# Output projection of a hybrid decoder layer: activations held in the array, 512 weight columns moving

## What is computed

```python
mixed = concat([a * silu(ga), p * silu(gb)], axis=-1)           # 544 x 2048
h = (DEEPNORM_ALPHA * x + einsum('btc,cd->btd', mixed, w_out))  # w_out 2048 x 2048
mu = mean(h); var = mean(square(h - mu))
y = (h - mu) * rsqrt(var + LN_EPS) * ln_g + ln_b
```

## Time and profile before

| | |
|---|---|
| median of 3 runs | 1218.41 us |
| the profiled execution | 1214.59 us |
| its span in the trace | 1212.5 us |
| matmuls busy | 1179.9 us, 97% |
| first matmul of stage D | 983.23 us |
| last matmul of stage D ends | 1186.75 us |

### The profile page before, as it was taken

One profiled execution on the slowest core, in us unless ns is written; L12 is line 12 of the kernel. 1 busy time (PEld: TensorE's weight loads), 2 busy tenths in 40 slices (PEclk: granted clock), 3 DMA queues, 4 the chain that ended last, 5 costly groups with the idle time before them and its releaser, 6 DMA issues.

```text
span 1212.5 us, 26754 instructions
## 1 busy us (share of the span) xinstructions
PE 1179.9 (97%) x10300; PEld 1087.3 (90%) x10300; DVE 597.2 (49%) x1083; ACT 359.0 (30%) x665; POOL 354.1 (29%) x150
## 2 busy tenths in 40 slices
PE   6999999999999999999989999999999999999995
PEld 6888889999999999999987889888889879999992
DVE  3666658874665657451444622623523552323226
ACT  4333333223323323322333322322323342122210
POOL 2432222333333334334311311311321223333310
PEclk9999999999999999999999999999999999999996
DMA  7543143233232223354226857857867656222203
GB/s 250 130 121 80 48 111 89 70 88 89 79 104 82 80 79 98 93 154 129 62 85 196 287 208 245 300 194 250 287 207 248 214 189 219 82 76 86 69 1 147
DMA packets 197975, 170.50 MB, mean 141 GB/s; under 512 B 19890, under 2 KB 178538, under 8 KB 196658
## 3 DMA queue, kind: packets, MB, share of 16 engines
q1 hardware_dynamic: 184458, 160.48, 42.7%
q10 hardware_dynamic: 13424, 8.67, 2.4%
HBM read 159.47 MB, written 9.74 MB: 140 GB/s over the span
## 4 chain that ended last, share of the span: by engine, by line
PE 91%; DVE 6%; issue 1%; DMA 1%; ACT 1%; DVEq 0%; SPq 0%; ACTq 0%
PE acc L1138 67%; PE bank L1438 5%; PE bank L1454 3%; PE acc L1525 3%; PE bank L1196 2%; PE bank L1332 2%; PE bank L1313 2%; DVE scoreP L1793 1%; PE acc L1579 1%; DVE top L1789 1%; PE acc L1483 1%; DMA xnat<-in_x_prompt 1%; PE bank L1248 1%; DVE y L2185 1%; PE bank L1322 1%
## 5 line engine op out<-in xcount | busy, mean ns | idle before, releaser
L634 POOL TENSOR_TENSOR wL<-rawW,wH 128x1024 fp32r<-128x1024 f32 (+1 forms) x146 | 353.9, 2425 | 811.4 <-ACT wH L656 811.4
L1138 PE MATMUL acc<-actH,wH 128*128 128x272 f32 (+1 forms) x2304 | 491.5, 294 | 1.2 <-DVE actL L1707 1.2
L1138 PE MATMUL acc<-actH,wL 128*128 128x272 f32 (+1 forms) x2304 | 476.6, 288 | 0.0
L1138 PE MATMUL acc<-actL,wH 128*128 128x272 f32 (+1 forms) x2304 | 475.0, 288 | 0.0
L1138 PEld LDWEIGHTS acc<-actH,wH 128*128 128x128 f32 (+1 forms) x2304 | 360.1, 188 | 23.9 <-issue 21.9
L1138 PEld LDWEIGHTS acc<-actL,wH 128*128 128x128 f32 (+1 forms) x2304 | 361.4, 188 | 0.0
L1138 PEld LDWEIGHTS acc<-actH,wL 128*128 128x128 f32 (+1 forms) x2304 | 359.1, 188 | 0.0
L656 ACT ACTIVATE wH<-rawW 128x1024 fp32r<-128x1024 f32 (+1 forms) x146 | 153.7, 1054 | 226.2 <-PE acc L1138 210.3
L2120 DVE SCALAR_TENSOR_TENSOR y<-y,bank 128x512 f32 (+1 forms) x16 | 11.0, 688 | 122.3 <-PE bank L1647 120.4
L1438 PE MATMUL bank<-sq,kPage 128*128 128x128 f32 x480 | 65.6, 280 | 4.1 <-DVE kPT L1951 4.0
L1438 PEld LDWEIGHTS bank<-sq,kPage 128*128 128x128 f32 x480 | 52.9, 142 | 14.5 <-issue 9.8
(11 more groups left out here) (207 smaller groups left out, 1019.6 us busy)
## 6 DMA issues: line engine op xcount, KB each, us to landing
rawW<-in_w_in SPq DMA_DIRECT2D x112, 512.0 KB, 3.8
vPage<-in_cache_v SPq DMA_DIRECT2D x64, 512.0 KB, 4.8
kPage<-in_cache_k SPq DMA_DIRECT2D x60, 512.0 KB, 4.6
rawW<-in_w_out SPq DMA_DIRECT2D x32, 512.0 KB, 4.1
y<-in_x_prompt SPq DMA_DIRECT2D x4, 1024.0 KB, 9.3
out_y_prompt<-y SPq DMA_DIRECT2D x8, 512.0 KB, 2.8
xnat<-in_x_prompt SPq DMA_DIRECT2D x2, 1024.0 KB, 7.9
xnat<-in_x_prompt ACTq DMA_DIRECT2D x2, 1024.0 KB, 10.9
```

The lines of the kernel that those rows point to most:

```text
L634: pool.tensor_tensor(wL[:, slot, :, 0:width], rawW[:, slot, :, 0:width], wH[:, slot, :, 0:width].bitcast(F32), ALU.subtract).then_inc(stag ...
L1138: last = pe.matmul(acc[t.slot][0:width, e, 0:HT], w[:, u.slot, k, 0:width], a[:, kk, e * HT:(e + 1) * HT], start=(half == 0 and k == 0 and ...
```

## The change

In the output projection the operands change places. The activations of one token tile (128 channels by 128 tokens) are the stationary operand, and 512 weight columns move. The output has 4 blocks of 512 columns (`BLOCKS`, `WIDE`). A weight unit is now 2 chunks by 512 columns, still 512 KB, 8 units to a block, in the order `PAIRS`. For each unit and each of the 4 prompt token tiles there are 2 x 3 = 6 matmuls of 512 columns; the sums lie in four banks of PSUM, tokens on the partitions, and no transposes follow.

The 32 samples are not taken in three products but in one fp32 product of `mixed` with `rawW`: `sample_parts` puts 128x32 weights into the four column groups, one chunk to each, with 512 columns of `rawW` moving, once for each two units. The four partial sums stand on 128 partitions; ACT copies them out (`part_copy`), and `folded` adds them by a matmul with four identities side by side (`fold`, 128x32). As TensorE now reads `rawW`, SP waits for `pair_done` of the two units that had the slots before, where it waited for POOL; ACT waits for `pair_done` too.

The first eight units are taken in the last pass of `group` and after it, where `first_tile` was. On SP the units 4 to 7 of `w_out` stand after the pages of V and ahead of the loads of x. `gbc` has memory of its own.

In the last block the token tiles end one after another, and DVE, ACT and TensorE do the normalization of a tile while TensorE multiplies for the next: `normal`, `finished`, `shift_turned`, `correction`, in the order `NORMED` (tiles 0, 1, samples, 2, 3).

```diff
+WIDE = 4 * P
+BLOCKS = D // WIDE
+PAIRS = (4, 5, 6, 7, 0, 1, 2, 3)
+NORMED = (0, 1, TT, 2, 3)
...
+            def load_out_unit(t, n, col, done):
+                if done is None:
+                    sp.wait_ge(stage_ready[t.slot], t.free)
+                else:
+                    sp.wait_ge(pair_done, done)
+                stand_alone(sp)
+                sp.dma_start(rawW[:, t.slot].rearrange("p k c -> p (k c)").rearrange("p (k c) -> p k c", k=2),
+                             wo_view[:, 2 * PAIRS[n]:2 * PAIRS[n] + 2, ds(col, WIDE)]).then_inc(w_landed[t.slot], 16)
...
-                    load_unit(wo_view, 1 - half, (tile - 4) * P, t)
+                    load_out_unit(t, j - 8, 0, None if j < 12 else (j - 12) // 2 + 1)
...
                 for m in range(PAGES):
-                    if m % 2 == 0:
+                    if m % 2 == 0 and not last:
                         unit(12 + m // 2, last, g)
...
             group(LOOPS, True)
+            for j in range(12, 16):
+                unit(j, True, LOOPS)
...
-                for j in range(2):
-                    load_tile(wo_view, (2 * i + 4 + j) * P, TILE_D + 4 + j, i, 2)
+                for n in range(8):
+                    load_out_unit(turn(2 * TILE_D + 8 + n, 4, i, 8), n, (i + 1) * WIDE, 4 * i + (n + 4) // 2 + 1)
...
+            def out_high(n):
+                u = out_unit(n)
+                act.wait_ge(w_landed[u.slot], 16 * u.full)
+                act.wait_ge(pair_done, (n - 4) // 2 + 1)
+                act.activation(wH[:, u.slot, :, :], rawW[:, u.slot, :, :], ACT.Copy).then_inc(high_ready[u.slot], 1)
...
+            for n in range(4, 8 * BLOCKS):
+                if n % 8 == 2 and n > 8:
+                    part_copy(n // 8 - 1)
+                out_high(n)
...
+            def rows_times(q, t, n, first=False, last=False):
+                for c in range(2):
+                    k = 2 * PAIRS[n % 8] + c
+                    for w, parts in ((wH, (actH, actL)), (wL, (actH,))):
+                        for a in parts:
+                            end = pe.matmul(out_bank(q), a[:, k, t * P:(t + 1) * P], wide(w, n, c),
+                                            start=first and c == 0 and w is wH and a is actH,
+                                            stop=last and c == 1 and w is wL)
...
+            def sample_parts(p):
+                q = 5 * (p // 4) + TT
+                weights_ready(2 * p + 1)
...
+                for j in range(4):
+                    n, c = 2 * p + j // 2, j % 2
+                    end = pe.matmul(out_bank(q)[NS * j:NS * (j + 1), :], mixed[:, 2 * PAIRS[n % 8] + c, NP_:T], wide(rawW, n, c),
+                                    start=p % 4 == 0, stop=p % 4 == 3, skip_group_check=True)
+                end.then_inc(pair_done, 1)
...
+                pe.matmul(out_bank(5 * b + TT)[0:NS, :], fold[:], raw[:, b % 2, 0:WIDE], start=True, stop=True
+                          ).then_inc(fold_full, 1)
...
                     if last and m == 5:
-                        first_tile(range(8, 12), (0, 1))
+                        out_tiles(0)
                     if last and m == 7:
-                        first_tile(range(12, 16), (0, 1))
+                        out_tiles(1)
+                        sample_parts(0)
                     value_page("b", m)
                 if last:
-                    first_tile(range(0, 4), (0,))
+                    out_tiles(2)
                     output_turned("b")
-                    first_tile(range(4, 8), (0,))
-                    first_tile(range(0, 8), (1,))
+                    out_tiles(3)
+                    sample_parts(1)
...
+            for n in range(4, 8 * BLOCKS - 4):
+                out_tiles(n)
+                if n % 2:
+                    sample_parts(n // 2)
+                if n % 8 == 0:
+                    folded(n // 8 - 1)
...
+            a, b, c, d = range(8 * BLOCKS - 4, 8 * BLOCKS)
+            first = 5 * (BLOCKS - 1)
+            weights_ready(a)
+            weights_ready(b)
+            sample_parts(4 * BLOCKS - 2)
+            for t in range(2):
+                rows_times(first + t, t, a)
+                rows_times(first + t, t, b)
+            weights_ready(c)
+            rows_times(first, 0, c)
+            weights_ready(d)
+            rows_times(first, 0, d, last=True)
+            sample_parts(4 * BLOCKS - 1)
+            rows_times(first + 1, 1, c)
+            rows_times(first + 1, 1, d, last=True)
+            folded(BLOCKS - 1)
+            rows_times(first + 2, 2, a)
+            shift_turned(0)
+            rows_times(first + 2, 2, b)
+            rows_times(first + 2, 2, c)
+            correction(0)
+            rows_times(first + 2, 2, d, last=True)
+            rows_times(first + 3, 3, a)
+            shift_turned(1)
+            rows_times(first + 3, 3, b)
+            correction(1)
+            rows_times(first + 3, 3, c)
+            shift_turned(2)
+            rows_times(first + 3, 3, d, last=True)
+            correction(2)
+            for at in (3, 4):
+                shift_turned(at)
+                correction(at)
...
+            normal(0)
+            normal(1)
+            normal(2)
+            finished(0)
+            normal(3)
+            finished(1)
+            finished(2)
+            normal(4)
+            finished(3)
+            finished(4)
```

More of the change, by code:

```diff
@@ L1467, in new_keys @@
                 full(b, last)
[L1469 to L1489, removed]
@@ new lines, in rows_times @@
+            def rows_times(q, t, n, first=False, last=False):
[6 more added lines that the diff above has]
+                                            stop=last and c == 1 and w is wL)
+                if last:
+                    end.then_inc(out_full, 1)
@@ L1491, in _, with folded @@
+            def folded(b):
+                pe.wait_ge(gb_clear, 1)
+                pe.wait_ge(part_copied, b + 1)
+                pe.matmul(out_bank(5 * b + TT)[0:NS, :], fold[:], raw[:, b % 2, 0:WIDE], start=True, stop=True
+                          ).then_inc(fold_full, 1)
             copied(TILE_C + 31)
@@ L1636, in _ @@
                 group(g, g == LOOPS)
[L1637 to L1669, removed]
@@ new lines, in shift_turned, with correction @@
+            def shift_turned(at):
+                t = NORMED[at]
+                m = P if t < TT else NS
+                pe.wait_ge(shift_ready, at + 1)
+                if at:
+                    pe.wait_ge(shift_copied, at)
+                else:
+                    pe.wait_ge(out_read, 17)
+                pe.transpose(out_bank(16)[:, 0:m], shift[0:m, t, :], ident[0:m, 0:m]).then_inc(shift_full, 1)
+            def correction(at):
+                t = NORMED[at]
+                m = P if t < TT else NS
+                pe.wait_ge(shift_copied, at + 1)
+                if at == 0:
+                    pe.wait_ge(gb_in, 16 * 8)
+                for j in range(4):
+                    if at:
+                        pe.wait_ge(y_ready, 4 * (at - 1) + j + 1)
+                    pe.matmul(out_bank(12 + j)[0:m, :], shiftT[32 * j:32 * j + 2, t * P:t * P + m], gb[32 * j:32 * j + 2, :],
+                              start=True, stop=True).then_inc(corr_full, 1)
@@ L2111, in _ @@
             own.step(dve.memset(shift[:].rearrange("p t (j c) -> p t j c", j=4)[:, :, :, 1], 1.0))
+            own.step(dve.tensor_tensor(fold[:], ident[:, 0:NS], ident[:, NS:2 * NS], ALU.add))
+            for j in (2, 3):
+                own.wait()
+                own.step(dve.tensor_tensor(fold[:], fold[:], ident[:, NS * j:NS * (j + 1)], ALU.add))
+            own.wait()
             dve.wait_ge(y_in, 16 * (TT + 1))
@@ L2141, in _ @@
-            with dve.Fori(0, KC // 2 - 1) as i:
-                own.enter(i, 2 * (TT + 3))
-                for j in range(2):
-                    residual(2 * i + j, j, i)
-                    statistics(2 * i + j)
-                    gained(2 * i + j)
-                own.leave(KC // 2 - 1)
-            own.step(dve.memset(mv[:], 1.0))
-            for j in range(2):
-                residual(KC - 2 + j, j, KC // 2 - 1)
-                statistics(KC - 2 + j)
-                if j == 0:
-                    gained(KC - 2)
@@ L2170, in _ @@
[L2170 to L2186 removed]
+            reads = 0
@@ new lines, in added @@
+            def added(b, t):
+                nonlocal reads
+                m = P if t < TT else NS
+                if t < TT:
+                    dve.wait_ge(out_full, TT * b + t + 1)
+                else:
+                    dve.wait_ge(fold_full, b + 1)
+                at = y[0:m, t, b * WIDE:(b + 1) * WIDE]
+                dve.scalar_tensor_tensor(at, at, ALPHA, out_bank(5 * b + t)[0:m, :], ALU.mult, ALU.add).then_inc(out_read, 1)
+                reads += 1
+                dve.wait_ge(out_read, reads)
+                own.step(dve.bn_stats(bn[0:m, t, b, :], at))
+                own.wait()
```

193 lines of the change are left out of this document (102 added, 91 removed).

## The result

The changed kernel took 1222.15 us (median of 8 runs, 1220.54 to 1223.47), the kernel before 1217.94 (8 runs, 1216.77 to 1219.67) beside it: ratio 1.0037, 95% interval 1.0027 to 1.0047. It is slower by 0.4%, 4.2 us, where 1215.3 and "faster" were forecast; 1222.15 lies just inside the range, whose end is 1222.5. The profiled execution took 1223.25 us with a span of 1221.4.

What follows compares the result with a forecast made beforehand. TensorE's own work was taken as the bound. Work -2.5, x's stop +6.0 and clock +1.6, last block +2.0, tail -10.2 summed to -3.1 us: 1215.3 us against the median of 1218.41, range 1207.5 to 1222.5.

Steps and rivals of the forecast that it cites:

- the price of a tile matmul: Stage D, 768 matmuls of 512 columns: 225.3 ns each, 173.0 us in all, with 166.1 and 181.1 as ends.
- The support from fp32: Reason given for 12.0 ns over the cycles belonging to each tile matmul: fp32 rows have a fixed surplus too.
- The rival on the other side: Tile matmuls' surplus goes by the column, 235.8 ns each: 6.0 us more, 1221.3 us, slower; chance 0.25.
- the forecast -3.1: Whole kernel: sum of all terms, -3.1 us, giving 1215.3 us against the median of 1218.41; chance 0.42.
- Samples: Sixteen `sample_parts` in stage D: 1.19 us each including mode changes, 19.1 us on TensorE.
- `folded`: Four times in stage D, one full-height fp32 matmul adding the sample sums: 0.86 us each, 3.4 in all.
- The stop: TensorE idle before unit 8 of `w_out`, its weights behind x on SP's queue: 6.0 us, plus 1.6 for the clock.
- The climb taken from one row: Clock's recovery after TensorE's idle time before unit 8: 1.6 us, none at the low end, 3 at the high.
- Steady state: Weight units ready 7.9 and 10.3 us after `pair_done`, needed after 12.0 and 17.4: loads hidden, no wait.
- Last block: TensorE's waits for the last units' weights: 1.3 and 1.0 us, taken as 2.0 in all.
- Tail: From the last tile matmul to the end, bound by DVE: 15.6 us where it was 25.8, 10.2 less.
- the wait for `correction(2)`, 1.1: After the last tile matmul, DVE waits 1.1 us for this correction between `finished(1)` and `finished(2)`.

Runs made afterwards that it cites:

- experiment 1: Standalone kernel, nothing of the layer computed: 48 matmuls in a row at each of several widths; fp32r starts 119.8 ns apart at 256 columns, 227.3 at 512.
- the address streams: Standalone kernel, nothing of the layer computed: 512-column fp32r matmuls with blocks taken from other places of the tile; 227 ns at 512-byte multiples, 232.5 begun 128 bytes past.
- experiment 5: Changed kernel with stage D's activations packed in chunks of 512 columns, so every block begins at a multiple of 512 bytes: 1220.23 us, ratio 1.0018 to the kernel before.
- experiment 6: Changed kernel with x loaded in four pieces of 512 columns, the later ones behind the first two weight units of their block: 1214.66 us, ratio 0.9982.
- experiment 7: Changed kernel with 12 of 16 `sample_parts` each replaced by one transpose, so `y_sample` lacks those products: 1213.2 us, ratio 0.9959 to the kernel before.
- experiment 10: Changed kernel with one swap on ACT, `shift_copy(3)` ahead of `deviation(4)`: 1219.42 us, ratio 1.0015 to the kernel before.

## Why the prediction was wrong

**The step that failed first is the price of a tile matmul, "I take 225.3, the middle".** It measured 231.7 ns. Its two parts were nearly right: the cycles, and a surplus that belongs to each matmul and not to its columns (0.42 ns a column, experiment 1), 13 ns for 12. The support from fp32 was thin, as 512 columns of fp32 have only 2 to 3 ns over their cycles (429 ns a record in experiment 1). A part was missing. Before, blocks of weights that begin on multiples of 512 bytes were in the array; the change puts blocks of activations there, and in their chunks of 544 columns every other chunk begins 128 bytes off a multiple of 256. That costs 5 ns of 227, shown by the address streams and undone by packing. 6.4 ns over 768 matmuls are 4.9 us. The prediction swapped the operands and priced only their widths. The rival on the other side, over 230 ns, came within 1 us of the time (1221.3 for 1222.15) for a reason that the widths refute: that is luck.

This term alone turns the forecast -3.1 into +1.8 us, but it isn't all of the miss. Without the address cost the kernel is still slower than the one before (experiment 5: 1.0018, 2.2 us); two smaller terms, `folded` and the tail, were short as well.

**Samples: right.** 1.00 us and 0.2 in the matmuls behind, for 1.19. **`folded`: 0.3 short.** 0.97 and again 0.2 behind it, 1.17 for 0.86; four times, 1.2 us. The change of mode that was priced for the samples was forgotten here.

**The stop: right.** 5.1 us and 1.9 of clock, for 6.0 and 1.6; the path was the one described, and experiment 6 takes it away. The climb taken from one row is a middle at best: in the traces of experiments 5 and 7 it is 2.4 and 3.0 us. The stop is shorter than forecast by about what the slower matmuls ahead of it took. **Steady state: right**, no other wait. **Last block: right**, the waits are 1.2 and 0.7 us for 2.0.

**Tail: 16.9 us for 15.6.** The sum has one wait of DVE, "the wait for `correction(2)`, 1.1", and none behind it. `correction(3)` was taken as hidden, but ACT's queue has `deviation(4)` ahead of its input, and DVE stood for 1.7 us. ACT's order was the one that the prediction did not walk through. With the two swapped (experiment 10) the tail is 15.2 us.

Against the forecast difference of -3.1 us: +4.9 (address and remaining surplus), +1.2 (`folded`), +1.3 (tail), -0.6 (stop and climb), -0.1 (last block) give +3.6; measured is +4.2, by an interval of 3.3 to 5.7. The remaining 0.6 is within the interval and not accounted for.

## What to carry to other kernels

When operands trade places between the array and the moving side, look at where each block begins in a partition as well as at its width: here chunks of 544 fp32 values cost 2% on the 512-column matmuls of the stage, and a repacking of what was copied anyway gave it back. When a bulk load that nothing needs soon is moved, compare it with the next load that something does need, in the same queue; cut into the pieces in which it is used, it no longer stopped TensorE. And a gain ahead of a stop is no gain until the stop is gone: what experiment 7 saved in the two pairs ahead of it came back as a longer wait and a longer climb, and samples first alone only moved a wait.

## What the runs showed of the hardware that was not expected

- A 128x128 fp32r block in the array that begins off a multiple of 256 bytes in its partition: 232 to 233 ns a matmul of 512 columns, for 227, and 232 when only every other chunk is off. Moving columns that begin 128 bytes off: 233. Narrower matmuls didn't show it: 272 columns whose moving operand begins 0, 16 and 64 bytes off take 125.4, 124.3 and 126.6 ns, and 256 columns with every other chunk in the array off take 119 ns, as with none off.
- fp32r has 12 to 14 ns over its cycles and bf16 3, at 272 as at 512 columns; 448 columns of fp32r have 20 and 496 have 17, unexplained.
- At half clock neither is seen: behind the stop matmuls of 512 columns, misaligned blocks among them, start 426 to 427 ns apart, which is 512 columns at 1.2 GHz (estimate: 426.7).
- Each passage between full-height fp32r and fp32, in column groups or not, costs 0.2 us in the matmuls that follow.
